# Three gate products in the woven groups of RWKV and six beside S5, instead of two and seven

## The chip, the cores and the metric

The kernel runs on one core of a Trainium2 chip. A core has five engines with instruction queues of their own: TensorE (PE, matrix products into PSUM banks; PEld is its loading of weights), VectorE (DVE), ScalarE (ACT), GpSimd (POOL) and SyncE (SP), which here issues nearly all DMA transfers. Engines wait for each other by semaphores. The metric is the device time of one execution in microseconds (us), the median of several. Lower is better.

## The reference, cut to what matters

The program is two layers of a network on 256 tokens of width 2048, in float32. The change lies in the second layer. It normalizes its input to `h`, projects it, and feeds three branches (GDN, RWKV, S5), which are merged under gates:

```python
h = rms_norm_2(x, norm_w[i])
proj = h @ w_in[i]
(g_qkv, g_z, g_b, g_a, r_feat, r_z, s_u, s_z, gate_logits) = _split_cols(proj, SPLIT_SIZES)
o_a = gdn_branch(...)      # gated delta rule, chunks of tokens
o_b = rwkv7_branch(...)    # state recurrence over tokens, 16 heads of 64
o_c = s5_branch(...)       # complex diagonal recurrence over 256 tokens
branch_proj = einsum('blnc,ncd->blnd', branches, w_branch[i])
gates = sigmoid(gate_logits.reshape(bsz, seq, N_BRANCH, D_MODEL) + gate_b[i])
merged = sum(gates * branch_proj, axis=2)
x = x + merged @ w_out[i]
```

The gates depend on `h` alone, so their products can be made at any time before the merge. They are 3 branches x 2048 columns; in chunks of 512 columns that is 12 gate products, each 256 tokens x 2048 x 512.

## The kernel before

The second layer runs as `stage_gdn`, `stage_rwkv`, `stage_s5`, `stage_merge`, one after the other. Within a stage the engines run `nc.Block`s: every engine has its list of instructions, and all engines meet at the end of a block. Nothing in a stage starts before the block ahead of it is over on every engine.

The class `Beside` makes products with the whole of `h` (kept in SBUF as `whole`, named `x_rows` in the profile) in small pieces beside the work of a stage. A job is one chunk of 512 columns: a gate product or one of the four chunks of the S5 input. It has 8 units; a unit is 2 row tiles x 2 slices of the contraction, 4 matmuls of 128x512, which the profile shows as 8 records since each float32 matmul is done in two passes. A gate job begins with two matmuls that put the bias into its two banks (4 records, L3244). `on_pe(pe, units)` is written out by hand in PE's program and issues so many units (L3249). A job takes two PSUM banks. When its last unit is done, `on_act` empties both on ACT (L3265, a sigmoid for gates), and SP stores the result to DRAM (L3216). The weights of a unit are one DMA (L3210) into a ring of 5 slots.

The 12 gate jobs are dealt out by two constants: `GATES_BESIDE_GDN = 3` in GDN, `GATES_BESIDE_RWKV = 2` in RWKV, and the other 7 in S5. The RWKV stage also makes the four S5 input chunks, so its list of jobs is three S5 chunks, the gate jobs, and the last S5 chunk.

The third block of `stage_rwkv` (called the woven block below) holds the RWKV recurrence as 4 groups (2 halves of the heads x 2 row tiles). A group needs the inverse of a triangular matrix (`Inverse`: `turn`, then five levels of `masked_products` and `update_products`, L3048 and L3059), and with it two chunks of recurrence (`key_state` L4035/L4036, `solved` L4044, `read_out` L4057 to L4066). PE weaves the recurrence of group n into the inverse of group n+1. Between them stand units of the jobs, by the table

```python
BEFORE_FIRST, IN_GROUP, BEHIND_LAST = 3, (1, 1), ((1, 1, 2), (1, 1, 1))
```

3 units before the first inverse; in each of the three groups one in slot 0 (before `solved(n, 0)`) and one in slot 1 (before level 5 of the inverse); and 4 + 3 in the six slots of the last group's recurrence, which has no inverse beside it. 3 + 6 + 7 = 16 units are 2 jobs. In this block the jobs have a ring of only two banks of their own (`banks[6:8]`, `beside.ring`), which is what one job takes; ACT also copies the inverse's products to SBUF (L3104).

`stage_s5` has a first block (coefficients, and one gate job on PE in three pieces) and a second, the recurrence. There PE makes the inputs of the recurrence (L4509), then `beside.on_pe(pe, (len(jobs) - 1) * Beside.UNITS)`, six gate jobs in a row, and then the output products (L4519), eight tiles of the state to a bank, four banks. DVE runs `s5_scan` meanwhile; its last loop goes in 8 steps over 4 tiles each (L4282 to L4289, 128x960), and each step raises `s_dve`, on which the output products wait. After the scan DVE reads the four banks (L4550), ACT applies GELU to the whole (L4533), and the block ends. The next block loads `s5_glu_w` (L240) and multiplies by it (L257).

Of the kernel before, what the change touches and what calls it, by code (L numbers as in the profile page):

```python
# [3269 lines left out]
def gate_jobs(io, gates_dram, lo, hi):  # L3270

    work = [(br, c) for br in range(BRANCHES) for c in range(D // CHUNK)][lo:hi]
    return [(io["w_in_2"][0], MG0 + br * D + c * CHUNK, io["gate_b_2"][0, br:br + 1, c * CHUNK:(c + 1) * CHUNK], ACT.Sigmoid,
             gates_dram[br, c]) for br, c in work]


GATES_BESIDE_GDN = 3
GATES_BESIDE_RWKV = 2

GDN_PARTS = (4, 3, 5, 4, 4, 2, 2)  # L3280

# [1 line left out]

SHIFT_UNITS = 10

BEFORE_FIRST, IN_GROUP, BEHIND_LAST = 3, (1, 1), ((1, 1, 2), (1, 1, 1))


GH, GD = 8, 128
# [431 lines left out]
def stage_rwkv(nc, m, io, st, whole, cols, s5_dram, gates_dram):  # L3721
    with ExitStack() as ctx:
# [20 lines left out]
        s5_jobs = [(io["w_in_2"][0], SU0 + c * CHUNK, None, ACT.Copy, s5_dram[c]) for c in range(4)]  # L3743
        rwkv_jobs = s5_jobs[0:3] + gate_jobs(io, gates_dram, GATES_BESIDE_GDN, GATES_BESIDE_GDN + GATES_BESIDE_RWKV) + s5_jobs[3:4]
        beside = Beside(m, st, ctx, "s5_in", whole, rwkv_jobs)
# [19 lines left out]
        with ExitStack() as c1:  # L3765
# [4 lines left out]
            with nc.Block() as block:  # L3770
                @block.sync
                def _(sp):

                    beside.load_units(sp, 2)
                    sp.wait_ge(fed_stored, 16 * (1 + TT * len(chunks(NP_, RWKV_WIDTH))))
                    for tt in range(TT):
                        sp.dma_start(prev[:, tt, :], fed[tt * P:(tt + 1) * P, 0:NR]).then_inc(shifted[tt], 16)
                    beside.load_units(sp, 3)
                    sp.dma_start(mu, everywhere(io["rwkv_mu_2"], NR)).then_inc(mu_loaded, 16)
                    beside.on_sp(sp, 1)  # L3780
                    sp.dma_start(wup[:, 0, :], io["rwkv_w_up_2"][0]).then_inc(up_loaded, 16)
                    sp.dma_start(wup[:, 1, :], io["rwkv_a_up_2"][0]).then_inc(up_loaded, 16)
                    for (row, name), landed in zip(rows_of, (r_loaded, r_loaded, kk_loaded, ka_loaded, rk_loaded)):
                        sp.dma_start(row, everywhere(flat(io[name]), HALF)).then_inc(landed, 16)
                    beside.load_units(sp, SHIFT_UNITS + 1)
                    beside.store(sp)
# [177 lines left out]
        with ExitStack() as c2:  # L3964
# [7 lines left out]
            groups = [(hg, tt) for hg in range(2) for tt in range(TT)]  # L3972
            with nc.Block() as block:
                @block.sync
                def _(sp):
                    beside.on_sp(sp, GATES_BESIDE_RWKV)
                    beside.load_units(sp, beside.at_unit + Beside.HELD)
# [7 lines left out]
                @block.scalar  # L3985
                def _(act):
                    for n in range(len(groups)):
                        inv.at(n)
                        if n == len(groups) - 1:
                            beside.on_act(act)  # L3990
                        for lv in range(1, inv.LEVELS + 1):
                            inv.copy_products(act, lv)
                    beside.on_act(act)

                @block.tensor
                def _(pe):
# [331 lines left out]
def stage_s5(nc, m, io, st, whole, cols, s5_dram, gates_dram):  # L4328
    with ExitStack() as ctx:
# [6 lines left out]
        par = m.sb(ctx, "s5_parity", [P, 2])  # L4336
        jobs = gate_jobs(io, gates_dram, GATES_BESIDE_GDN + GATES_BESIDE_RWKV, BRANCHES * (D // CHUNK))
        beside = Beside(m, st, ctx, "s5_gates", whole, jobs)
# [442 lines left out]
```

## Time and profile before

| | us |
|---|---|
| median of 3 runs | 3711.11 (3708.2 to 3716.0) |
| the profiled execution | 3712.48 |
| its span in the trace | 3710.5 |
| woven block of RWKV, from the first transposes to the last unit | 2859.0 to 3103.7 |
| second block of S5, from the first input product to the end of GELU | 3185.7 to 3399.2 |

In the whole span PE is busy 90%, DVE 70%, ACT 34%, POOL 11%. These are averages over stages with different limits. Times below are us from the start of the span. A row of the timeline gives start, duration, engine, line, operation, output and inputs, the shape, the number of instructions merged into the row, and in brackets how long the engine had been idle and for whom. A matmul's duration runs to the end of its pipeline, so neighbouring matmuls overlap a little, and the distance of two starts is the better price.

### The profile page before, as it was taken

Reading aid. Unit: us, or ns where it says so; the run is one execution under the profiler, and the core shown is the slowest. Engines: PE = TensorE matmul, PEld = TensorE weight load, DVE = VectorE, ACT = ScalarE, POOL = GpSimd, SP = SyncE. Lnnn points to the kernel's source line nnn. Section 1 sums busy time; section 2 is a strip of 40 time slices with the busy share of each in tenths; the row PEclk is TensorE's granted clock in tenths of the full one; section 3 lists DMA queues with packets and bytes.
Section 4 is the critical chain, followed back from the end, with each engine's and each line's share of the span. In section 5 each row is a group of like instructions: output and inputs, shape, how many; then the busy total and the mean of one; then the engine's idle time right before and its main releaser. Section 6 shows DMA issues by size and latency. Waiting matters only on the chain. (4 is left out here: it accounts for less than half of the span.)

```text
span 3710.5 us, 46494 instructions
## 1 busy us (share of the span) xinstructions
PE 3355.6 (90%) x18811; PEld 2618.5 (71%) x18811; DVE 2597.8 (70%) x3306; ACT 1267.8 (34%) x1467; POOL 410.6 (11%) x393
## 2 busy tenths in 40 slices
PE   7889878998889989999999799998989998999798
PEld 5756646788889989787877588567864764543676
DVE  5855768889999987687888754756446334894664
ACT  3322233334345555444444333313312010100333
POOL 0011101100121121232332100020000200000000
PEclk8888988999999999999999999999999989999899
DMA  9974367847989999899999564315563104453663
GB/s 355 379 266 131 115 221 286 304 166 257 328 317 368 364 352 353 334 380 373 366 379 385 220 209 155 115 41 169 199 219 108 42 19 118 149 152 103 206 230 147
DMA packets 294612, 870.29 MB, mean 235 GB/s; under 512 B 33584, under 2 KB 108436, under 8 KB 242432
## 3 DMA queue, kind: packets, MB, share of 16 engines
q1 hardware_dynamic: 257616, 670.64, 51.5%
q0 software_dynamic: 34320, 190.40, 13.6%
q10 hardware_dynamic: 2464, 6.29, 0.5%
q8 instruction: 149, 2.44, 0.3%
q14 instruction: 63, 0.52, 0.0%
HBM read 820.22 MB, written 46.38 MB: 234 GB/s over the span
## 5 line engine op out<-in xcount | busy, mean ns | idle before, releaser
L2493 DVE TENSOR_TENSOR expert_w_low<-expert_w,expert_w_high 128x2048 fp32r<-128x2048 f32 x256 | 585.4, 2287 | 154.3 <-ACT expert_w_high L2920 151.9
L2828 PE MATMUL bank<-h_halves,expert_w_high 128*128 128x384 f32 x2048 | 611.3, 369 | 64.8 <-DVE expert_w_low L2493 64.5
L2920 ACT ACTIVATE expert_w_high<-expert_w 128x2048 fp32r<-128x2048 f32 x256 | 490.4, 1916 | 449.7 <-DMA expert_w<-in_peer_v_dram 295.6
L298 DVE TENSOR_TENSOR weights_low<-weights,weights_high 128x1024 fp32r<-128x1024 f32 (+4 forms) x288 | 338.3, 1177 | 297.1 <-ACT weights_high L281 293.5
L2829 PE MATMUL bank<-h_halves,expert_w_low 128*128 128x192 f32 x2048 | 520.2, 254 | 0.0
L281 ACT ACTIVATE weights_high<-weights 128x1024 fp32r<-128x1024 f32 (+4 forms) x288 | 293.5, 1021 | 468.1 <-PE bank L326 384.7
L2828 PEld LDWEIGHTS bank<-h_halves,expert_w_high 128*128 128x128 f32 x2048 | 394.0, 192 | 75.3 <-DVE expert_w_low L2493 75.0
L2829 PEld LDWEIGHTS bank<-h_halves,expert_w_low 128*128 128x128 f32 x2048 | 400.6, 196 | 0.0
L2897 PE MATMUL bank<-expert_w_high,gated_acts_halves 128*128 128x512 f32 x512 | 203.4, 397 | 22.6 <-DVE expert_w_low L2493 22.5
L2898 PE MATMUL bank<-expert_w_low,gated_acts_halves 128*128 128x512 f32 x512 | 201.5, 394 | 0.0
L2899 PE MATMUL bank<-expert_w_high,gated_acts_halves 128*128 128x512 f32 x512 | 201.5, 393 | 0.0
L2901 PE MATMUL bank<-expert_w_high,gated_acts_halves 128*128 128x512 f32 x512 | 199.2, 389 | 0.0
L2902 PE MATMUL bank<-expert_w_low,gated_acts_halves 128*128 128x512 f32 x512 | 199.2, 389 | 0.0
L3249 PE MATMUL bank<-s_gates_w,x_rows 128*128 128x512 f32 x448 | 198.2, 603 | 0.4 <-DMA s_gates_w<-in_w_in_dram 0.4
L3249 PE MATMUL bank<-s_in_w,x_rows 128*128 128x512 f32 x384 | 185.2, 640 | 11.5 <-DMA s_in_w<-in_w_in_dram 8.8
L3249 PEld LDWEIGHTS bank<-s_gates_w,x_rows 128*128 128x128 f32 x448 | 85.5, 192 | 111.2 <-issue 109.9
L3249 PEld LDWEIGHTS bank<-s_in_w,x_rows 128*128 128x128 f32 x384 | 77.0, 205 | 111.0 <-issue 96.3
L2789 POOL DMA_INDIRECT query_area<-in_peer_v_dram,own_list x43 | 114.8, 2671 | 260.1 <-DVE choose_area L2549 253.1
L1495 PE MATMUL bank<-weights,x_rows 128*128 128x512 f32 (+1 forms) x256 | 121.9, 630 | 18.6 <-DMA weights<-in_w_in_dram 15.3
L324 PE MATMUL bank<-weights_high,branch_high 128*128 128x512 f32 x320 | 127.7, 399 | 11.4 <-DVE weights_low L298 6.8
L2897 PEld LDWEIGHTS bank<-expert_w_high,gated_acts_halves 128*128 128x128 f32 x512 | 97.3, 190 | 50.5 <-issue 30.7
L326 PE MATMUL bank<-weights_high,branch_low 128*128 128x512 f32 x320 | 125.8, 393 | 0.0
(740 smaller groups left out, 6508.1 us busy)
## 6 DMA issues: line engine op xcount, KB each, us to landing
expert_w<-in_peer_u_dram SPq DMA_DIRECT2D x128, 1024.0 KB
expert_w<-in_peer_v_dram SPq DMA_DIRECT2D x128, 1024.0 KB
weights<-in_ada_w_dram SPq DMA_DIRECT2D x88, 512.0 KB, 9.3
weights<-in_w_out_dram SPq DMA_DIRECT2D x32, 1024.0 KB, 13.3
weights<-in_w_in_dram SPq DMA_DIRECT2D x32, 960.0 KB, 9.1
weights<-in_w_in_dram SPq DMA_DIRECT2D x32, 928.0 KB, 9.8
weights<-in_w_in_dram SPq DMA_DIRECT2D x56, 512.0 KB, 7.1
s_gates_w<-in_w_in_dram SPq DMA_DIRECT2D x56, 512.0 KB, 3.7
```

The costliest lines, as they stand in the source:

```text
L281: act.activation(self.high[:, u % self.UNITS_HELD, :, 0:n], self.buf[b][:, k:k + self.UNIT, 0:n], ACT.Copy).then_inc(self.high_ready, 1)
L298: dve.tensor_tensor(self.low[:, u % self.UNITS_HELD, :, 0:n], self.buf[b][:, k:k + self.UNIT, 0:n], self.high[:, u % self.UNITS_HELD, :, 0 ...
L2493: dve.tensor_tensor(wl[:, n % RING, :], w_sb[:, n % RING, :], wh[:, n % RING, :], ALU.subtract).then_inc(wl_ready, 1)
L2828: pe.matmul(o[:, 0:2 * DENSE], uh[:, b, k, :], acts.both[:, k, :, 0:DENSE], start=(k == 0), stop=False)
L2829: mm = pe.matmul(o[:, DENSE:2 * DENSE], ul[:, b, k, :], acts.h[:, k, 0:DENSE], start=False, stop=(k == KD - 1))
L2897: pe.matmul(bank[:, :], high, wh[:, b, cs], start=first, stop=False)
L2898: pe.matmul(bank[:, :], high, wl[:, b, cs], start=False, stop=False)
L2899: mm = pe.matmul(bank[:, :], low, wh[:, b, cs], start=False, stop=last)
L2901: pe.matmul(bank[:, :], both, wh[:, b, cs], start=first, stop=False)
L2902: mm = pe.matmul(bank[:, :], both, wl[:, b, cs], start=False, stop=last)
L2920: act.activation(wh[:, n % RING, :], w_sb[:, n % RING, :], ACT.Copy).then_inc(wh_ready, 1)
L3249: mm = pe.matmul(self.both[tt][:, :], self.whole[:, p * self.UNIT + u, tt * P:(tt + 1) * P], self.w[:, n % self.HELD, u, :], start=first, ...
```

## The change

One gate job goes from the second block of S5 to the woven block of RWKV. The 8 units are put where the table says: one more in both slots of each of the three groups, and one more in the first slot of each of the two chunks behind the last group. The list becomes 3 + 12 + 9 = 24 units, 3 jobs. ACT empties the first job's banks one group earlier, and two jobs at the end.

```diff
 GATES_BESIDE_GDN = 3
-GATES_BESIDE_RWKV = 2
+GATES_BESIDE_RWKV = 3
...
-BEFORE_FIRST, IN_GROUP, BEHIND_LAST = 3, (1, 1), ((1, 1, 2), (1, 1, 1))
+BEFORE_FIRST, IN_GROUP, BEHIND_LAST = 3, (2, 2), ((2, 1, 2), (2, 1, 1))
...
                 def _(act):
                     for n in range(len(groups)):
                         inv.at(n)
-                        if n == len(groups) - 1:
+                        if n == len(groups) // 2:
                             beside.on_act(act)
                         for lv in range(1, inv.LEVELS + 1):
                             inv.copy_products(act, lv)
-                    beside.on_act(act)
+                    for _job in range(GATES_BESIDE_RWKV - 1):
+                        beside.on_act(act)
```

What else follows from the constants: the woven block's SP list has one job more (8 weight loads, a bias load, a store) and the second block of S5 one less. The diff adds one line, so lines of the RWKV and S5 stages beyond it are one higher after the change (L4044 is L4045).

PE in the first woven group, slot 0 and what follows it (L4015 are the key products, L4044 is `solved`, L3059 `turn`, L3048 the first level). Here x4 counts matmuls, of which the trace shows two records each. Before:

```order
9916 L4015 MATMUL bank<-weights_3 64x128 x16
9917 L4036 MATMUL bank<-rwkv_rows,weights_3 64x64 x8
9918 L4015 MATMUL bank<-weights_3 64x128 x16
9919 L3249 MATMUL bank<-s_in_w,x_rows 128x512 x4
9920 L4044 MATMUL bank<-rwkv_xu,weights_3 64x64 x8
9921 L3059 MATMUL bank<-block_ident,weights_3 64x64 x16
9922 L3048 MATMUL bank<-weights_3 64x64 x16
```

PE in the same place of the changed kernel:

```order
9916 L4016 MATMUL bank<-weights_3 64x128 x16
9917 L4037 MATMUL bank<-rwkv_rows,weights_3 64x64 x8
9918 L4016 MATMUL bank<-weights_3 64x128 x16
9919 L3249 MATMUL bank<-s_in_w,x_rows 128x512 x8
9920 L4045 MATMUL bank<-rwkv_xu,weights_3 64x64 x8
9921 L3059 MATMUL bank<-block_ident,weights_3 64x64 x16
9922 L3048 MATMUL bank<-weights_3 64x64 x16
```

Two units stand where one was, and nothing else moved.

PE in slot 0 of the second woven group of the changed kernel, where the first job ends and the second begins in the same slot:

```order
10051 L4016 MATMUL bank<-weights_3 64x128 x16
10052 L3249 MATMUL bank<-s_in_w,x_rows 128x512 x4
10053 L3244 MATMUL bank<-s_in_bias,incl_mask 128x512 x2
10054 L3249 MATMUL bank<-s_in_w,x_rows 128x512 x4
10055 L4045 MATMUL bank<-rwkv_xu,weights_3 64x64 x8
```

Before, a job ended in one slot and the next began in another; now two ends of jobs lie within a slot, here and in the first slot behind the last group.

ACT in the woven block of the changed kernel (L3104 copies the inverse's products, ten to a group; L3265 empties a job's two banks):

```order
665 L3104 ACTIVATE rwkv_products<-bank 128x256 x20
666 L3265 ACT_TABLE_LOAD
667 L3265 ACTIVATE s_in_out<-bank 128x512 x2
668 L3104 ACTIVATE rwkv_products<-bank 128x256 x20
669 L3265 ACTIVATE s_in_out<-bank 128x512 x4
```

The first emptying stood behind 30 copies and stands now behind 20; two stand at the end, where one was.

PE at the end of the S5 recurrence of the changed kernel (L4520 are the output products, L4519 before the change):

```order
10408 L3244 MATMUL bank<-s_gates_bias,incl_mask 128x512 x2
10409 L3249 MATMUL bank<-s_gates_w,x_rows 128x512 x32
10410 L3244 MATMUL bank<-s_gates_bias,incl_mask 128x512 x2
10411 L3249 MATMUL bank<-s_gates_w,x_rows 128x512 x32
10412 L4520 MATMUL bank<-weights_3,s_C_T 32x256 x64
```

Five such pairs of rows stand ahead of the output products, where six were.

## Rows read from the trace of the kernel before

**Rows 1.** Stretches: bounds, length, busy us of each engine (instructions), PE's granted clock, DMA.

```profile
core 0: us, PE busy (x) PEld busy (x) DVE busy (x) ACT busy (x) POOL busy (x), PEclk, DMA share, GB/s
2904.00:3104.00 200.00, 191.59 (x2586) 136.56 (x2576) 60.44 (x124) 14.75 (x35) 22.22 (x18) 0.91 0.13 36
```

**Rows 2.** Timeline of PE in the first woven group.

```profile
2903.67 1.10 PE L4015 MATMUL bank<-weights 64*64 64x128 f32 x32 [0.23 <-DVE weights L4129]
2904.70 3.70 PE L3249 MATMUL bank<-s_in_w,x_rows 128*128 128x512 f32 x8
2908.33 1.08 PE L4044 MATMUL bank<-rwkv_xu,weights 64*64 64x64 f32 x15
...
2917.68 0.68 PE L3048 MATMUL bank<-weights,rwkv_products 64*64 64x64 f32 x16 [0.99 <-DVE rwkv_K L4170]
...
2940.01 5.76 PE L3249 MATMUL bank<-s_in_w,x_rows 128*128 128x512 f32 x8
2945.71 1.15 PE L3048 MATMUL bank<-weights,rwkv_last_masked 64*64 64x64 f32 x32
```

**Rows 3.** Timeline of DVE around slot 0 of the same group.

```profile
2904.80 0.68 DVE L4141 TENSOR_SCALAR rwkv_xu<-bank 64x512 f32<-64x512 f32 x1
2905.62 1.29 DVE L4120 TENSOR_TENSOR weights<-bank,block_masks 128x512 f32<-128x512 f32 x2
2909.51 0.68 DVE L4147 COPY rwkv_xu<-bank 64x512 f32<-64x512 f32 x1 [2.60 <-PE bank L4044]
```

**Rows 4.** Timeline of PE: one whole gate job beside the S5 recurrence, and the next.

```profile
3201.36 27.73 PE L3249 MATMUL bank<-s_gates_w,x_rows 128*128 128x512 f32 x64
3229.35 1.95 PE L3244 MATMUL bank<-s_gates_bias,incl_mask 1*128 1x512 f32 x4 [0.26 <-issue]
3231.23 27.73 PE L3249 MATMUL bank<-s_gates_w,x_rows 128*128 128x512 f32 x64
```

**Rows 5.** Timeline of PE between two jobs in the two-bank ring, second block of RWKV.

```profile
2830.31 27.70 PE L3249 MATMUL bank<-s_in_w,x_rows 128*128 128x512 f32 x64 [0.73 <-ACT s_in_out L3265]
```

**Rows 6.** Timeline of ACT: the first woven job is emptied.

```profile
3004.70 1.28 ACT L3265 ACT_TABLE_LOAD   x1 [6.02 <-PE bank L3249]
3006.00 1.08 ACT L3265 ACTIVATE s_in_out<-bank 128x512 f32<-128x512 f32 x2
```

**Rows 7.** Timeline of PE in the third group's slot 1 and behind the last group.

```profile
3037.75 3.77 PE L3244 MATMUL bank<-s_in_bias,incl_mask 1*128 1x512 f32 x4
3041.46 6.24 PE L3249 MATMUL bank<-s_in_w,x_rows 128*128 128x512 f32 x8
...
3055.73 5.93 PE L3249 MATMUL bank<-s_in_w,x_rows 128*128 128x512 f32 x8
...
3073.65 8.94 PE L3249 MATMUL bank<-s_in_w,x_rows 128*128 128x512 f32 x16
```

**Rows 8.** Timeline of PE at the end of the S5 recurrence.

```profile
3354.12 27.73 PE L3249 MATMUL bank<-s_gates_w,x_rows 128*128 128x512 f32 x64
3382.11 14.09 PE L4519 MATMUL bank<-weights,s_C_T 128*32 128x256 f32 x128 [0.26 <-issue]
```

**Rows 9.** Timeline of DVE in the same stretch.

```profile
3368.12 1.16 DVE L4282 TENSOR_TENSOR s_tmp_dve<-s_powers,s_carry 128x960 f32<-128x960 f32 x1
...
3375.86 1.15 DVE L4289 TENSOR_TENSOR weights<-weights,s_tmp_dve 128x960 f32<-128x960 f32 x1
3385.88 0.87 DVE L4550 SCALAR_TENSOR_TENSOR branch_columns<-s_u_columns,vector_columns,bank 128x256 f32<-128x256 f32 x2 [8.87 <-PE bank L4519]
...
3396.28 0.87 DVE L4550 SCALAR_TENSOR_TENSOR branch_columns<-s_u_columns,vector_columns,bank 128x256 f32<-128x256 f32 x2 [2.60 <-PE bank L4519]
```

**Rows 10.** Timeline of ACT behind that.

```profile
3397.24 1.91 ACT L4533 ACTIVATE branch_columns<-branch_columns 128x2048 f32<-128x2048 f32 x1 [13.37 <-DVEq L4553]
```

**Rows 11.** Timeline of PE in the block after it.

```profile
3403.25 16.53 PE L257 MATMUL bank<-weights,branch_columns 128*128 128x512 f32 x32 [7.05 <-DMA weights<-in_s_glu_w_dram]
3420.07 13.97 PE L257 MATMUL bank<-weights,branch_columns 128*128 128x512 f32 x32 [0.29 <-issue]
```

**Rows 12.** Stretches of PE's clock as it falls idle behind the output products.

```profile
3392.00:3396.00 4.00, 4.00 (x40) 1.00 0.00 0
3396.00:3400.00 4.00, 0.20 (x4) 0.77 0.00 0
3400.00:3404.00 4.00, 0.75 (x1) 0.50 0.88 277
```

## The prediction

> **What bounds the kernel now.** The change takes work from one place and puts it in another, so two places decide, and I read each for the engine that ends last. The table of the whole span (PE 90% busy) does not answer this; the stretches and the timelines do.
>
> First the S5 recurrence, where a job is taken away. Read the ends. PE starts its sixth gate job at 3354.12, which takes 27.73, and starts the output products at 3382.11 [rows 8]. DVE ends the last step of the recurrence at 3375.86 + 1.15 = 3377.0 and then waits 8.87 for PE's first bank [rows 9]. So PE is late, by 3382.1 - 3377.0 = 5.1 us at the start of the output products, and the products themselves (14.09) then run wholly behind the recurrence, though three quarters of them need only steps that had long ended. The chain there is: PE gate jobs, PE output products, DVE's last bank (ends 3396.28 + 0.87 = 3397.15 [rows 9]), GELU at 3397.24 [rows 10], end of the block.
>
> Then the woven block of RWKV, where the job goes. In the 200 us from 2904 to 3104 PE is busy 191.6, DVE 60.4, ACT 14.8, POOL 22.2 [rows 1]. PE is the bound, with only 8.4 us idle. What the reader should look for is whether this idle time lies where the new units stand. It does not. In slot 0 of the first group PE comes to the unit after the key products, runs it in 3.63 us from start to start (2904.70 to 2908.33), and goes on to `solved` without a gap [rows 2]. What `solved` waits for, DVE's negated rows, was ready at 2904.80 + 0.68 = 2905.5, and DVE had finished the value rows too (2905.62 + 1.29 = 2906.9) and sat idle 2.60 until PE's `solved` [rows 3]. The one unit already covers all that DVE had to do. In slot 1 the unit is followed by level 5 without a gap (2940.01, then 2945.71) [rows 2]. PE's waits in a group, 0.99 us for DVE before an update being the largest [rows 2], come further behind a unit, in a ping-pong of PE, ACT and DVE that starts anew after it, and a longer unit only shifts them.
>
> **What the change moves, term by term.**
>
> Units in the woven block. A whole job of 8 units takes 27.73 us [rows 4], 27.73 / 8 = 3.47 for a unit that directly follows another one; all 8 new units do. 8 x 3.47 = 27.7 us, all on PE's path. With the bias: two matmuls, from 3229.35 to 3231.23, 1.9 us [rows 4].
>
> Ends of jobs inside a slot. The two-bank ring makes PE wait until ACT has emptied both banks. The same ring cost 0.73 us between two jobs in the block before [rows 5]. There ACT needed no table load; here the first emptying is a sigmoid with a load of 1.28 ahead of it, on an ACT that had been idle for 6.02 [rows 6]. The first bank is full half a unit (1.7 us) before the second, so the load lies in that time. I take 0.73 twice, 1.5 us; bounds 1.1 (hardly more than the drain of 0.26 that every end has [rows 4] and one emptying) and 4.1 (two waits of 0.73, and two times 1.28 if the load or ACT's queue is not covered). Nothing else hangs on ACT there: its copies for the group ahead are done, those of the next come later.
>
> DMAs on SP: eight weight loads, a bias load and a store more in the woven block. The DMA engines are 13% busy there [rows 1], and a ring of five slots runs ahead of PE. Nothing, hidden behind PE's own units; if a load came late it would show as a PE wait, which no unit of the woven block has in the trace.
>
> Sum for RWKV: 27.7 + 1.9 + 1.5 = +31.1 us.
>
> S5. Without the sixth job PE is through 29.9 us earlier (3201.36 to 3231.23 is one job with bias and drain [rows 4]), at 3352.2. Then DVE is late: the recurrence does not depend on PE and still ends at 3377.0. A step of its last loop takes 8.9 us (3368.12 to 3377.0 [rows 9]) and an eighth of the products 14.09 / 8 = 1.8 [rows 8], so by 3377.0 the products of seven of eight steps are done, and after it PE has the last eighth left, 1.8 us at full clock. DVE meanwhile takes the first three banks, 0.87 each, then the fourth. The end is the later of DVE alone, 3377.1 + 4 x 0.87 = 3380.6, and PE's last eighth, 0.1 for the signal, 1.8 and 0.87 of DVE, 3379.8. At half the clock PE's eighth is 3.5 and the end 3381.5. Against 3397.15 that is 16.5 or 15.6 us. Which one? PE will have been idle for most of the 14 us ahead of it. The row for that: when PE fell idle at 3396.2 the clock went from 1.00 to 0.77 in the slice in which it stopped and to 0.50 (1.2 GHz) in the next [rows 12]. So I take the lower clock and 15.6. On this point the Trainium skill speaks against counting the full gain: "TensorE: Matmul & The Clock Gate", part 1, says that the throttled clock is the default and that only activity lifts it; the trace agrees as far as [rows 12] go, and by the rule the gain is 15.6, without it 16.5.
>
> Behind it: the load of the GLU weights is issued when the block is over, so the whole chain moves up. The first half of the GLU product took 16.53, the second 13.97, the difference 2.6 being the start at the low clock [rows 11]. It starts cold before and after; I count no difference, with +-1 us as bound. The scan itself, in DVE alone, keeps its time.
>
> Sum: +31.1 - 15.6 = **+15.5 us**. The profiled execution took 3712.48, its span 3710.5, with 2.0 around it that no edit touches; so 3728.0 for such an execution. It lies 1.4 above the median of the three runs. For the median: 3711.11 + 15.5 = **3726.6 us**, 0.42% slower. A job of 29.9 us is taken from a place that can give only half of it back, since the recurrence becomes the bound there, and put where PE has no idle time for it.
>
> **Rivals.**
>
> *The clock is kept up in RWKV (not slower).* The woven block runs at a mean clock of 0.91. Between the two levels of 1.2 and 2.4 GHz that is (1 - 0.91) x 2 x 200 = 36 us at the lower one. Slots with a dense unit came out at 5.76 [rows 2], 6.24 and 5.93 us [rows 7] instead of 3.70, and a bias pair at 3.77 [rows 7] instead of 1.9. The clock falls in long runs of small 64-wide products and comes back during a unit. If twice as many units keep it up, time comes back: at most half of the 36 us, 18, if everything in it were bound by columns. Then the block pays 31.1 - 18 = 13.1, and the total is -2.5: 3708.6, inside 0.2%. If a third comes back (6), it is 3720.6. The page named above has this rule too, activity releases the throttle, and by it a denser block should have fewer low stretches. What the rows say against it: the falls come far behind a unit, in read-out and key-state products whose length the change leaves alone; two units back to back still met one (8.94 instead of 3.63 + 3.47 = 7.1 [rows 7]). It decides for "not slower" from 8.1 us given back, for "faster by over 0.2%" only from 23, more than its ceiling.
>
> *The new units run at the low clock (slower still).* If the low stretches last through the whole slot, a new unit costs about 5.9 instead of 3.47, 2.4 more. For all eight that is +19 (3746), for half of them, those in slot 1 and the first behind, +10: 3736. Against it: two units in one slot took 8.94, not 12 [rows 7].
>
> *S5 gives less.* PE is late at the start of the output products by 5.1 us, and that much comes back in any case; the other 10.5 come back only if the products of the early steps do run during the recurrence. If half of that failed, 10 us would come back and the time is 3732. No row names what could hold them up: the four banks of this ring are empty and the weights are in SBUF.
>
> *The units fill waits after all.* If all 8.4 us of idle PE in the woven block were used up, the sum is +7.1 and the time 3718. [rows 2, 3] show the waits elsewhere.
>
> **How the numbers follow.** The sum as forecast, with the woven cost between 26 and 36: 0.66. Clock kept up by 6 us or more: 0.15 (of it 0.10 within 0.2%, 0.02 faster, 0.03 slower). Units at the low clock: 0.12. S5 gives less: 0.05. Waits filled: 0.02. A measurement of this kernel can tell about 0.2% (7.4 us) from no change. So faster 0.02, same 0.12, slower 0.86. The range reaches from 3716 (a clock that gives back 10 of its 18) to 3737 (half of the new units at the low clock); outside lie the rest of the first rival and the far end of the second, some 0.15 together.
>
> **What the profile after would show.** Right: in slots 0 and 1 rows of 16 records instead of 8, some 7.1 us long and up to 9.5 at a low clock, followed at once by the next products; the stretch from the first transposes to the last unit longer by about 31 us, with PE's idle time in it near 8 to 10 us; two waits of about 0.7 for ACT (L3265) on PE; in S5 PE idle between 3352 and 3377 on the old scale, rows of the output products split by waits for DVE, DVE's four readings right behind the recurrence, and GELU 15 to 16 us earlier relative to the first input product. Wrong: a mean clock in the woven block near 1.00, or PE's idle time in it fallen to a few us, or a recurrence that itself takes another time. If the woven block grew by less than 24 us, the first term is wrong; if S5 shrank by less than 13, the last.

## The result: 17.4 us slower

| | us |
|---|---|
| median before (14 runs beside the changed kernel) | 3710.28 (3693.71 to 3724.80) |
| median after (14 runs) | 3729.89 (3712.38 to 3738.59) |
| ratio after / before | 1.0047, 95% interval 1.0031 to 1.0063 |
| the profiled execution of after, and its span | 3718.94, 3717.0 |

The ratio is +17.4 us (11.5 to 23.4) on 3710.28; the forecast was +15.5 and a median of 3726.6. The measured median is 3.3 above the forecast, inside its range.

The two profiled executions differ by only 6.5 us in span. So the span as a whole must not be read; the stages must. The stages are cut at six starts that both traces have: the first transposes of the woven block (L371, `rwkv_K`), the next block's first unit, the transposes behind that block's job (L371 again), the first input product and GELU in S5's second block, and the transposes behind the GLU (L371, `s_y_rows`).

| us | before | after | difference |
|---|---|---|---|
| all that lies ahead of the woven block | 2859.0 | 2847.9 | -11.1 |
| woven block of RWKV | 245.8 | 279.4 | +33.6 |
| last block of RWKV | 28.0 | 28.0 | 0.0 |
| S5, first block | 52.8 | 55.0 | +2.2 |
| S5, second block up to GELU | 211.6 | 194.7 | -16.9 |
| GELU and GLU | 49.7 | 48.8 | -0.9 |
| the rest | 263.5 | 263.2 | -0.3 |

The code ahead of the woven block is the same in both kernels, and that part took 2845 to 2859 us in the traces of this case, whatever the kernel. So the 11 us lie inside the spread between executions, and they hid that much of the loss. From the woven block to the end the trace gives +17.6, and the runs give +17.4. How well a single trace can carry that is looked at under "The same again".

### The profile page after: what moved, and what is told of

Its sections match the earlier page's. It is cut to its first block and busy times, and to the rows that moved or that the text cites. A ratio compares the mean times of both kernels' runs of the same rounds, so it can differ in the third digit from the quotient of the medians.

```text
span 3717.0 us, 46494 instructions
## 1 busy us (share of the span) xinstructions
PE 3360.2 (90%) x18811; PEld 2623.0 (71%) x18811; DVE 2598.2 (70%) x3306; ACT 1267.2 (34%) x1467; POOL 410.5 (11%) x393
## 5 line engine op out<-in xcount | busy, mean ns | idle before, releaser
L3249 PE MATMUL bank<-s_in_w,x_rows 128*128 128x512 f32 x448 | 212.4, 632 | 12.1 <-DMA s_in_w<-in_w_in_dram 9.4
L3249 PEld LDWEIGHTS bank<-s_in_w,x_rows 128*128 128x128 f32 x448 | 88.7, 202 | 125.5 <-issue 110.1
L3249 PE MATMUL bank<-s_gates_w,x_rows 128*128 128x512 f32 x384 | 174.1, 615 | 0.0
L3249 PEld LDWEIGHTS bank<-s_gates_w,x_rows 128*128 128x128 f32 x384 | 74.9, 197 | 98.1 <-issue 98.0
L324 PE MATMUL bank<-weights_high,branch_high 128*128 128x512 f32 x320 | 127.3, 398 | 11.6 <-DVE weights_low L298 6.8
```

What stands on the lines that cost most here:

```text
L3249: mm = pe.matmul(self.both[tt][:, :], self.whole[:, p * self.UNIT + u, tt * P:(tt + 1) * P], self.w[:, n % self.HELD, u, :], start=first, ...
```

## The profile after

The head of the page of after: span, and busy time of each engine.

```profile
span 3717.0 us, 46494 instructions
PE 3360.2 (90%) x18811; PEld 2623.0 (71%) x18811; DVE 2598.2 (70%) x3306; ACT 1267.2 (34%) x1467; POOL 410.5 (11%) x393
```

Nothing of the change can be read from these shares. The woven block can be read as a stretch (length, busy time of PE, PEld, DVE, ACT, POOL, PE's clock, DMA), first in the trace of before and then in that of after:

```profile
2859.00:3104.90 245.90, 233.15 (x3273) 167.32 (x3273) 84.46 (x170) 18.92 (x45) 29.61 (x24) 0.92 0.17 49
```

```profile
2847.90:3127.30 279.40, 266.48 (x3340) 183.69 (x3341) 84.41 (x170) 20.13 (x47) 29.59 (x24) 0.91 0.19 60
```

PE's idle time is 245.9 - 233.15 = 12.75 us before and 279.4 - 266.48 = 12.92 after. The added work went on top of everything else. The groups of PE's instructions in that block show of what it consists. Before:

```profile
L3249 PE MATMUL bank<-s_in_w,x_rows 128*128 128x512 f32 x129 | 69.4, 691 | 1.2 <-PEq L3973 1.2
L4065 PE MATMUL bank<-rwkv_xu,weights 64*64 64x64 f32 x128 | 20.5, 247 | 0.0
L4044 PE MATMUL bank<-rwkv_xu,weights 64*64 64x64 f32 x128 | 9.0, 220 | 0.3 <-issue 0.3
L3244 PE MATMUL bank<-s_in_bias,incl_mask 1*128 1x512 f32 x8 | 5.8, 854 | 0.0
```

And after:

```profile
L3249 PE MATMUL bank<-s_in_w,x_rows 128*128 128x512 f32 x192 | 98.1, 667 | 0.0
L4066 PE MATMUL bank<-rwkv_xu,weights 64*64 64x64 f32 x128 | 21.4, 256 | 0.0
L4045 PE MATMUL bank<-rwkv_xu,weights 64*64 64x64 f32 x128 | 9.0, 220 | 0.0
L3244 PE MATMUL bank<-s_in_bias,incl_mask 1*128 1x512 f32 x12 | 5.9, 608 | 1.6 <-ACT s_in_out L3265 1.6
```

One of the 129 records of before belongs to the next block's unit (0.7 us), so the units went from 68.7 to 98.1, +29.4 us for 64 records. The bias went from 5.8 to 5.9 only, since one of its pairs had fallen into a low-clock stretch before [rows 7] and none did after. The new waits for ACT are 1.6 us.

The timeline of PE in the slots of after: slots 0 and 1 of the first group, slot 0 of the second group, where a job ends within the slot (its bias, with the wait), slot 1 of the third group, and the second end of a job, in the first slot behind the last group.

```profile
2893.54 7.13 PE L3249 MATMUL bank<-s_in_w,x_rows 128*128 128x512 f32 x16
2900.60 1.08 PE L4045 MATMUL bank<-rwkv_xu,weights 64*64 64x64 f32 x15
...
2932.91 8.70 PE L3249 MATMUL bank<-s_in_w,x_rows 128*128 128x512 f32 x16
...
2949.75 3.70 PE L3249 MATMUL bank<-s_in_w,x_rows 128*128 128x512 f32 x8
2954.30 1.95 PE L3244 MATMUL bank<-s_in_bias,incl_mask 1*128 1x512 f32 x4 [0.85 <-ACT s_in_out L3265]
2956.18 5.40 PE L3249 MATMUL bank<-s_in_w,x_rows 128*128 128x512 f32 x8
...
3051.01 9.38 PE L3249 MATMUL bank<-s_in_w,x_rows 128*128 128x512 f32 x16
...
3075.02 1.95 PE L3244 MATMUL bank<-s_in_bias,incl_mask 1*128 1x512 f32 x4 [0.73 <-ACT s_in_out L3265]
```

The first row answers to the unit of [rows 2]: 2893.54 to 2900.60 is 7.06 us instead of 3.63, and `solved` follows without a gap. 7.1 us is a pair at the high clock; 8.70 and 9.38 are pairs that met a low stretch, as the 8.94 of [rows 7].

The end of the S5 recurrence in after, PE and then DVE and ACT:

```profile
3378.55 10.61 PE L4520 MATMUL bank<-weights,s_C_T 128*32 128x256 f32 x96 [0.26 <-issue]
3392.69 1.94 PE L4520 MATMUL bank<-weights,s_C_T 128*32 128x256 f32 x16 [3.54 <-DVEq L4546]
3401.62 1.96 PE L4520 MATMUL bank<-weights,s_C_T 128*32 128x256 f32 x16 [6.99 <-DVEq L4546]
```

```profile
3400.37 1.15 DVE L4290 TENSOR_TENSOR weights<-weights,s_tmp_dve 128x960 f32<-128x960 f32 x1
3401.67 3.22 DVE L4551 SCALAR_TENSOR_TENSOR branch_columns<-s_u_columns,vector_columns,bank 128x256 f32<-128x256 f32 x8
```

```profile
3404.97 1.91 ACT L4534 ACTIVATE branch_columns<-branch_columns 128x2048 f32<-128x2048 f32 x1 [24.67 <-DVEq L4554]
```

In [rows 8] PE was late and did all the products in one row behind the recurrence. Now it has done six of eight parts early and waits for the scan before each of the last two; DVE reads the four banks in 3.22 us without a gap, where it waited 8.87 and 2.60 for PE in [rows 9]. From the end of the last step (3401.52) to GELU it is 3.5 us; before it was 3397.24 - 3377.01 = 20.2. The difference is 16.8 us.

## The experiments

The ratios are against before, from runs beside it on the same chip. Where a stage is named, its length comes from the trace of that kernel. Lengths of the two blocks in every trace, and what remains of the span from the woven block on:

| kernel | woven block | S5, second block | woven block to end |
|---|---|---|---|
| before | 245.8 | 211.6 | 851.5 |
| after | 279.4 | 194.7 | 869.1 |
| rwkv_alone | 279.3 | 213.2 | 885.7 |
| s5_alone | 245.3 | 194.6 | 837.9 |
| one_heap | 276.6 | 194.7 | 864.8 |
| unwoven1 | 245.6 | 213.3 | 851.7 |
| s5_two_less | 246.1 | 194.7 | 832.6 |
| change_again | 285.7 | 194.7 | 875.9 |
| rwkv_alone2 | 282.8 | 213.3 | 892.8 |

### The two halves apart

**rwkv_alone.** The woven block of the change, with seven jobs in S5 as before. Nothing of the result is left out; S5 makes one gate product a second time, into memory that nobody reads. The cut shows what it adds to the changed kernel.

```diff
 GATES_BESIDE_RWKV = 3
 BEFORE_FIRST, IN_GROUP, BEHIND_LAST = 3, (2, 2), ((2, 1, 2), (2, 1, 1))
...
+        spare = m.dram("spare_gate", [P, TT, CHUNK])
+        jobs = [jobs[0][:4] + (spare[:, :, :],)] + jobs
```

> The RWKV half of the change alone: three gate jobs in the woven block as after the change, and still seven in S5 (one of them is made a second time, into a spare buffer). Theory: PE bounds the woven block and nothing covers the eight new units, so it grows as it did after the change (33.6 us between the first transposes and the next block's first unit; 31.1 by the sum ahead of the result), and S5 gives nothing back: slower by 33 us, ratio 1.009. Rival (the new units fill waits and half of the cost of the change comes from elsewhere): slower by under 20 us.

Measured: 1.0116 (1.0096 to 1.0136), 3750.43 against 3708.87; that is +43 us (36 to 50). Its trace gives +34.2 from the woven block to the end, with the woven block at 279.3.

**s5_alone.** The code of before, with one gate job fewer in S5. It leaves out the last of the twelve gate products; the merge reads its neighbour instead (the second pair of lines), so the merge does the same work.

```diff
-        jobs = gate_jobs(io, gates_dram, GATES_BESIDE_GDN + GATES_BESIDE_RWKV, BRANCHES * (D // CHUNK))
+        jobs = gate_jobs(io, gates_dram, GATES_BESIDE_GDN + GATES_BESIDE_RWKV, BRANCHES * (D // CHUNK) - 1)
...
-                    sp.dma_start(gate[:, i % 3, :, :], gates_dram[br, c // CHUNK]).then_inc(gate_loaded[i % 3], 16)
+                    sp.dma_start(gate[:, i % 3, :, :], gates_dram[br, min(c // CHUNK, 2) if br == 2 else c // CHUNK]).then_inc(gate_loaded[i % 3], 16)
```

> The S5 half alone: two gate jobs in RWKV as before the change, six in S5; the last gate product is left out, and the merge reads its neighbour in its place. Theory: the recurrence on DVE becomes the bound and only about 16 us of a job's 29.9 come back: faster by 15.6 to 17 us, ratio 0.9955, DVE reading the four banks right behind its last step. Rival (PE's output products are held up otherwise): faster by 5 to 10 us. Rival (a job is worth its whole time): faster by 30.

Measured: 0.9946 (0.9929 to 0.9964), 3688.50 against 3708.87; -20 us (-26 to -13). The stages give -13.6, with the S5 block at 194.6 and a first block of S5 that took 57.4 instead of 52.8; the edit leaves that block alone, and it took 55.0 and 55.8 in other traces.

The two halves together give 43 - 20 = +23 by the medians and 34.2 - 13.6 = +20.6 by the stages, against 17.4 and 17.6 for the whole. The woven block and the second block of S5 are each the same whether the other half is there or not (279.4 and 279.3, 194.7 and 194.6). Without the edit the S5 block took 211.5 to 213.3, so its part is 17 to 18.6 us. Two of the medians lie farther out than the stages; **rwkv_alone2** looks at that again below.

### Does it matter how the third job is put in?

**one_heap.** The third job stands as a heap of eight more units ahead of the first group; the slots keep one unit each. ACT's emptying is moved to match. The cut is against the kernel before.

```diff
-GATES_BESIDE_RWKV = 2
+GATES_BESIDE_RWKV = 3
...
-BEFORE_FIRST, IN_GROUP, BEHIND_LAST = 3, (1, 1), ((1, 1, 2), (1, 1, 1))
+BEFORE_FIRST, IN_GROUP, BEHIND_LAST = 11, (1, 1), ((1, 1, 2), (1, 1, 1))
...
-                        if n == len(groups) - 1:
+                        if n in (0, len(groups) - 1):
                             beside.on_act(act)
```

> The change with its eight new units in one heap ahead of the first inverse, where nothing waits beside them, and the table of the groups as before it (one unit to a slot). ACT empties the first job ahead of the first group's copies. Theory (the second unit of a slot covers nothing): the same as the change, slower than before by 15 to 19 us; a little less, by the 2 us that low-clock stretches and one end of a job cost in the slots. Rival (weaving covers waits): the heap is slower than the change by 5 us or more.

Measured: 1.0023 (1.0007 to 1.0039), +8.5 us (2.6 to 14.5). That is less than the 15 to 19 us expected; the trace gives +13.3 from the woven block to the end. The woven block grew by 30.8, not by 33.6. Of the 2.8 less, 1.6 lie in the units (96.5 us instead of 98.1; 97.1 below holds one record of the next block) and 0.8 in the wait for ACT, which comes once instead of twice; the bias (+1.8) and the small products (-1.8) cancel. The stretch in this kernel,

```profile
2859.40:3136.10 276.70, 264.91 (x3341) 181.96 (x3341) 84.46 (x170) 20.13 (x47) 29.61 (x24) 0.92 0.19 61
```

and the two groups:

```profile
L3249 PE MATMUL bank<-s_in_w,x_rows 128*128 128x512 f32 x193 | 97.1, 658 | 1.2 <-PEq L3973 1.2
L3244 PE MATMUL bank<-s_in_bias,incl_mask 1*128 1x512 f32 x12 | 7.7, 772 | 0.8 <-ACT s_in_out L3265 0.8
```

A heap that lies beside nothing costs no more than eight units woven in. So the weaving of the third job hides none of it. If anything the heap is cheaper: its units run one behind the other at a granted clock of 1.00, and the units cost 27.8 us more than before, where the woven ones cost 29.4 here and 35.9 in a second trace below.

**unwoven1.** The two jobs of before, with the six units of the groups' slots put ahead of the first group too.

```diff
-BEFORE_FIRST, IN_GROUP, BEHIND_LAST = 3, (1, 1), ((1, 1, 2), (1, 1, 1))
+BEFORE_FIRST, IN_GROUP, BEHIND_LAST = 9, (0, 0), ((1, 1, 2), (1, 1, 1))
...
-                        if n == len(groups) - 1:
+                        if n == 0:
```

> The kernel before with the six units of the groups' slots (one each) taken out and put ahead of the first inverse, so that the groups hold none. Theory: the first unit of a slot does cover something, since DVE works for 1 to 2.3 us from PE's arrival at slot 0 and for about 3 at slot 1, which then shows as PE waits: slower than before by 3 to 12 us, PE idle in the woven block up by as much. Rival (no unit of a slot covers anything): the same time within 2 us. Together with the change this gives the worth of no, one and two units to a slot.

Measured: 1.0001 (0.9988 to 1.0015), and a woven block of 245.6 against 245.8. I had expected it to be 3 to 12 us slower, since the prediction reads [rows 2, 3] as a unit that covers DVE's work. It does cover it, but the wait that it covers is short. PE in slot 0 of the first group, without a unit between the key products and `solved`:

```profile
2917.10 1.10 PE L4015 MATMUL bank<-weights 64*64 64x128 f32 x32 [0.23 <-DVE weights L4129]
2919.02 1.08 PE L4044 MATMUL bank<-rwkv_xu,weights 64*64 64x64 f32 x15 [0.81 <-DVEq L4142]
```

The wait of 0.81 us is all that a unit of 3.6 us hides there; before `solved` PE waits 1.6 us in the whole block, and PE's idle time in it is 12.2 us against 12.7 before.

That the length is the same does not mean that the six units left no trace. PE's stretch from the start of the first inverse on, first before and then here, and this kernel's units as a group:

```profile
2884.30:3104.88 220.58, 209.66 (x3118) 153.66 (x3117) 70.54 (x147) 18.92 (x45) 22.22 (x18) 0.91 0.13 38
```

```profile
2898.90:3095.56 196.66, 187.07 (x3064) 150.73 (x3065) 70.32 (x147) 16.52 (x42) 22.25 (x18) 0.88 0.08 24
L3249 PE MATMUL bank<-s_in_w,x_rows 128*128 128x512 f32 x128 | 61.0, 632 | 0.0
```

The units cost 7.7 us less than in the kernel before (61.0 against 68.7) and the bias pairs 1.9 less (3.9 against 5.8), since more of them ran at the high clock. PE's other work took as much longer, some 10 us (168.5 against 158.6), in groups whose granted clock was 0.88 where it had been 0.91. These two cancel. **For the length of this block the table of the slots decides hardly anything: PE's work is its length, and moving units only moves who meets the low clock.** This rests on one trace of unwoven1; the medians agree that the time is the same.

### How much can S5 give?

**s5_two_less.** As s5_alone, with two jobs fewer: the last two of the twelve gate products are left out, and the merge reads another one in their places.

```diff
-        jobs = gate_jobs(io, gates_dram, GATES_BESIDE_GDN + GATES_BESIDE_RWKV, BRANCHES * (D // CHUNK))
+        jobs = gate_jobs(io, gates_dram, GATES_BESIDE_GDN + GATES_BESIDE_RWKV, BRANCHES * (D // CHUNK) - 2)
...
```

> The kernel before with two gate jobs fewer beside the S5 recurrence (five in S5; the last two gate products are left out, and the merge reads their neighbour). Theory: with one job fewer DVE's recurrence is already the bound of that block, so the second one fewer gives nothing: the block from the first input product to GELU takes 194.6 us as with one fewer (211.6 before), and the time is 17 us below before, no more. Rival (PE still bounds part of the block): another 5 to 30 us.

Measured: 0.9917 (0.9894 to 0.9941), 3683.90 in four runs. The block is 194.7 us, as with one job fewer. PE and ACT at its end:

```profile
3357.29 1.96 PE L4519 MATMUL bank<-weights,s_C_T 128*32 128x256 f32 x16 [7.16 <-DVEq L4545]
3366.22 1.96 PE L4519 MATMUL bank<-weights,s_C_T 128*32 128x256 f32 x16 [6.98 <-DVEq L4545]
```

```profile
3369.57 1.91 ACT L4533 ACTIVATE branch_columns<-branch_columns 128x2048 f32<-128x2048 f32 x1 [56.20 <-DVEq L4553]
```

The second job fewer gives nothing in its block: the scan sets the end, and with one job fewer PE already waits 3.54 and 6.99 us for it. The medians show -31 us (-39 to -22), and the block explains -16.9 of it; the trace's other stages from the woven block on give -2.0 more, to -18.9 in all. The trace does not show where the rest of the -31 comes from; there are only four runs.

### The same again

The woven block of before took 245.3 to 246.1 us in the five traces that have its units where they were. To see how firm the 279.4 is, the change itself and rwkv_alone were run once more.

**change_again** is the changed kernel, unaltered.

> The changed kernel once more, beside its RWKV half alone on the same chip. The stages of the traces add to 17.6 us over the kernel before: ratio 1.0047. Its woven block 279.4 us and its S5 block 194.7 in the trace.

Measured: 1.0045 (1.0029 to 1.0061), +16.7 us: the result stands. But its trace has a woven block of 285.7, 6.3 us longer, at a mean clock of 0.90. Its stretch, its units as a group, and some of its slots in the timeline:

```profile
2846.80:3132.50 285.70, 272.15 (x3341) 184.79 (x3341) 84.41 (x170) 20.12 (x47) 29.61 (x24) 0.90 0.19 59
```

```profile
L3249 PE MATMUL bank<-s_in_w,x_rows 128*128 128x512 f32 x193 | 105.3, 704 | 1.2 <-PEq L3973 1.2
```

```profile
2994.34 9.91 PE L3249 MATMUL bank<-s_in_w,x_rows 128*128 128x512 f32 x16
...
3067.04 5.97 PE L3249 MATMUL bank<-s_in_w,x_rows 128*128 128x512 f32 x8
...
3073.75 2.45 PE L3244 MATMUL bank<-s_in_bias,incl_mask 1*128 1x512 f32 x4 [0.73 <-ACT s_in_out L3265]
3076.13 6.55 PE L3249 MATMUL bank<-s_in_w,x_rows 128*128 128x512 f32 x8
```

More of the slots fell into low-clock stretches: 9.91 instead of 7.1 for a pair, 5.97 and 6.55 instead of 3.6 for single units. The units took 104.6 us (105.3 less the one record of the next block) where the same code took 98.1. The small products did not grow: none of their larger groups took longer than in the first trace (L4066, for one, 21.2 us against 21.4).

**rwkv_alone2** is rwkv_alone, unaltered.

> The RWKV half alone once more. Its first measurement was 1.0116 (1.0096 to 1.0136), 43 us, where the stages of its trace add to 34.2. If the stages tell the whole of it, the ratio is 1.009 now, and the difference to the changed kernel 17 us. If the half alone costs something ahead of RWKV that one trace does not show, the ratio is again near 1.0116 and the difference 25 us.

Measured: 1.0095 (1.0076 to 1.0114), +35 us (28 to 42), so the first +43 was probably some 8 us too high, which its interval (36 to 50) allows. Its trace gives +41.3 from the woven block on, with a woven block of 282.8 and a first block of S5 3.0 us longer than before; the first trace gave 34.2. A single trace of a kernel with three woven jobs is good to some 7 us. The distance to the change is 35 - 17 = 18 us, close to S5's part, 16.9 by the block.

### A version that is faster than both

The same units stand in GDN, too. In the block of GDN's recurrence four of them stand at the start (`GDN_PARTS[4]`), and DVE waits 10.24 us there for PE's first product; at the end PE waits 7.69 us for the last rows, with nothing to do. PE and DVE before, at the end and at the start:

```profile
2537.84 3.68 PE L371 MATMUL bank<-ident,gdn_rows 128*128 128x128 f32 x16 [7.69 <-DVEq L3700]
...
2546.11 0.74 PE L324 MATMUL bank<-weights_high,h_rwkv_high 128*128 128x480 f32 x1 [4.59 <-DVE h_rwkv_low L566]
```

```profile
2434.18 1.89 DVE L3628 COPY weights<-bank 128x512 f32<-128x512 f32 x3 [10.24 <-PE bank L3544]
```

**gdn_tail** moves two of the four units from the start to the end, ahead of that wait. ACT empties the job at the end, and its store goes behind the weight loads on SP.

```diff
-GDN_PARTS = (4, 3, 5, 4, 4, 2, 2)
+GDN_PARTS = (4, 3, 5, 4, 2, 2, 2, 2)
...
-                    beside.finish_sp(sp)
                     sp.wait_ge(o_ready, TT)
                     m.weights.load(sp, io["w_in_2"][0], RF0, RWKV_WIDTH)
+                    beside.finish_sp(sp)
...
-                        if c == TT - 1:
-                            beside.on_act(act)
...
+                    beside.on_act(act)
...
+                    beside.on_pe(pe, GDN_PARTS[7])
                     pe.wait_ge(o_done, 1)
```

> The kernel before, all computed, with two units of the third GDN gate job moved within GDN: out of the four ahead of the recurrence's block, where DVE waits 10.2 us for PE, and in front of the final transposes, where PE waits 7.7 us for DVE. ACT's emptying of that job and its store move to the end, behind the load of the RWKV weights. Theory (a unit costs nothing only where PE waits): faster by 6 to 7 us, ratio 0.998. Rival (a unit is worth the same everywhere): no change. Rival (the late store holds the block's end up): slower by 2 to 4.

Measured: 0.9978 (0.9964 to 0.9992), -8 us (-13 to -3), 3705.40 against 3712.63. PE at the end of that block and at the start of the next, the store on SP's queue, and DVE at the start:

```profile
2516.13 7.03 PE L3249 MATMUL bank<-gdn_gates_w,x_rows 128*128 128x512 f32 x16
2523.97 1.97 PE L371 MATMUL bank<-ident,gdn_rows 128*128 128x128 f32 x16 [0.82 <-DVEq L3700]
...
2535.56 0.74 PE L324 MATMUL bank<-weights_high,h_rwkv_high 128*128 128x480 f32 x1 [9.61 <-DVE h_rwkv_low L566]
```

```profile
2523.97 0.34 SPq L3216 DMA_DIRECT2D merge_gates<-gdn_gates_out  x1
```

```profile
2420.65 1.89 DVE L3628 COPY weights<-bank 128x512 f32<-128x512 f32 x3 [3.38 <-PE bank L3543]
```

The wait at the start fell by 6.9 and the units lie in what was idle time (7.69 to 0.82). But half of it is lost again behind it: from the last transposes to the next block's first product it takes 11.6 instead of 8.3 us, since the block is not over before the late store has landed (SP waits for it in `finish_sp`). The store is issued at 2523.97 and takes 7.6 us to land, and SP's first DMA of the next block is issued at 2532.12. In the trace the stage as a whole became only 0.5 us shorter (214.3 to 213.8), with 3.4 us more in an earlier part at a lower clock.

**gdn_tail_b** is the same with one unit more at the start of the stage, and one fewer in the third part.

```diff
-GDN_PARTS = (4, 3, 5, 4, 2, 2, 2, 2)
+GDN_PARTS = (5, 3, 4, 4, 2, 2, 2, 2)
```

> The same, and one unit of GDN's first block moved from its third piece (five units, behind which DVE waits 8.7 us) to its first, behind which PE waits 3.0 us in three places. Theory: another 3 us, faster than before by 9 to 10 us, ratio 0.9975. Rival (the first piece then delays DVE's softplus chain): no more than the run without it.

Measured: 0.9981 (0.9966 to 0.9995), -7 us (-13 to -2); its stage took 211.0. The 3 us more that were expected of it did not show; the two can't be told apart. Both are faster than before by 0.2%, and than the change by more. The stage explains only part of that: 0.5 us of 8 in the one trace and 3.3 of 7 in the other. Where the rest comes from is not shown.

## Why the prediction was right, point by point

**Units in the woven block: 27.7 forecast, 29.4 measured** in the trace of after (35.9 in that of change_again, by the groups). All lie on PE's path, as forecast. The step price of 3.47 us holds at the high clock: 2893.54 to 2900.60 is 3.63 + 3.43. What was missing is the clock. For woven units a forecast at the price of a dense job is the lower edge: some of them will fall into stretches at 1.2 GHz.

**Bias: 1.9 forecast, 0.1 in the trace.** The added pair cost 1.95, and another got cheaper by 1.8, having left a low stretch.

**Two ends of jobs inside a slot: 1.5 forecast, 0.85 + 0.73 = 1.6 measured.** The row of an idle ring at another place [rows 5] was a good price. The first end has 0.12 more, and a table load comes before its emptying; that the load is the cause is not shown.

**What the sum had left out: 3.8 us of small products.** PE's busy time grew by 33.3, the units and the bias by 29.5. The rest is spread over the read-out and key-state products, such as L4066 (20.5 to 21.4), and those of the inverse (L3048, where the three largest groups went from 69.4 to 71.5). At a mean clock of 0.92 over 245.9 us the block of before spent (1 - 0.92) x 2 x 245.9 = 39 us at 1.2 GHz, that of after at 0.91 some 50, so more low time fell on them too; the rounding of the clock is worth 2.5 us in these figures. The idle time stood at 12.9, with the 1.6 of new waits in it, so 1.4 of the old waits were filled.

**S5: 15.6 forecast, 16.9 measured.** The step that was a little off is the choice between 16.5 and 15.6. I took the lower clock at the last eighth to mean twice its time, 3.5 us. The clock was at the lower level, 1.2 GHz, as PE's stretches of after show (length, busy times, then the clock):

```profile
3392.00:3396.00 4.00, 1.94 (x16) 0.59 (x16) 3.86 (x5) 0.00 (x0) 0.00 (x0) 0.68 0.01 4
3400.00:3404.00 4.00, 1.96 (x16) 0.63 (x16) 3.85 (x8) 0.00 (x0) 0.00 (x0) 0.50 0.00 0
```

But the eighth took 1.96 us there, as it had taken 1.94 where the clock was 0.68 on average, and 14.09 / 8 = 1.76 in the unbroken row of before [rows 8]. So DVE was the later one, and its four banks (3.22) set the end. On this point "TensorE: Matmul & The Clock Gate", part 1, of the Trainium skill was right that an idle TensorE falls back to the throttled clock (0.50 in the row above), and I drew too much from it: these products did not take twice as long for that.

**The GLU: no difference forecast, -0.9 measured**, inside the bound of 1. The first half took 15.49 where it was 16.53 in [rows 11].

**The rivals.** *The clock is kept up* did not come true for the second unit of a slot: the mean clock was 0.91 and 0.90, not higher than the 0.92 of before, and the small products took more time, not less. Its mechanism is not empty, though. Without the first unit (unwoven1) the groups ran at 0.88 instead of 0.91 and their small products took longer, which cancelled what the units had gained outside. *The new units run at the low clock* holds in part: it was worth 2 to 8 us of the 19 it could have cost, by execution. The ceiling of 19 was itself too low. The 5.9 us a unit that it goes by were units only partly at the low clock (0.59 to 0.64 on average over the rows of 5.76 to 6.24); a unit wholly at 1.2 GHz would take 2 x 3.63 = 7.3 us, an estimate from the last section's rows. *S5 gives less* is refuted, since the products of the early steps ran during the recurrence (the row of 96). *The units fill waits* is refuted but for 1.4 us, and one_heap says the same: without any cover the job costs 30.8.

**How much of the closeness is luck.** The sum of after's stages is 33.6 - 16.9 = +16.7, and +0.9 from the small stages. The mechanism held in both places, but the 2 us between forecast and trace are what is left of misses that partly cancel: units +1.7, bias -1.8, waits +0.1, small products +3.8, old waits filled -1.4, S5 -1.3, small stages +0.9. In change_again the woven block grew by 39.9 us, beyond the 26 to 36 that the forecast allowed for it. That the woven cost varies by 6 us between executions while the ratios of two measurements agree (1.0047 and 1.0045) leaves open which of the two traces is the usual one; the medians speak for a sum of 17.

## What to carry to other kernels

Independent work is free only where the engine that does it waits. Before moving it, find for both places which engine ends last, and from what point another takes over: here a job of 30 us was worth 17 where the recurrence stood behind it, nothing from the second job on, and its full price plus waits where PE was the bound. A place with an instruction between two dependent ones is not proof that something is hidden: take the instruction away, or find the wait that it covers (here 0.8 us). And when a time stays the same, look whether its parts did: unwoven1 kept its length because units got cheaper by as much as other products got dearer. And where the span as a whole varies more than the edit is worth, compare stage by stage and add up.

## What the runs showed of the hardware

**A low granted clock does not slow all matmuls alike.** Rows as stretches, with the mean granted clock as the third number from the end: a woven unit of change_again (512 columns; 3.70 us at 1.00); key-state products of after, 18 records and then 14 (the x counts take in neighbours that overlap); and output products of S5 (256 columns into 32 rows) in s5_two_less, 32 records and then 16.

```profile
3067.04:3073.01 5.97, 5.97 (x9) 2.32 (x8) 0.68 (x1) 0.60 (x1) 0.00 (x0) 0.61 0.00 0
3063.47:3065.78 2.31, 2.31 (x18) 1.71 (x18) 0.00 (x0) 0.00 (x0) 0.00 (x0) 1.00 0.00 0
3065.78:3068.61 2.83, 2.83 (x17) 2.01 (x15) 0.00 (x0) 0.00 (x0) 0.00 (x0) 0.50 0.00 0
3311.60:3315.30 3.70, 3.67 (x32) 1.20 (x32) 3.56 (x4) 1.68 (x2) 0.00 (x0) 1.00 0.35 142
3330.10:3332.10 2.00, 1.96 (x16) 0.63 (x16) 1.94 (x2) 0.00 (x0) 0.00 (x0) 0.50 0.00 0
```

For the unit time and clock trade one for one: 5.97 x 0.61 = 3.6. A bias pair, also 512 columns, took 3.77 us at 0.50 [rows 7] and 1.95 at 1.00. The 64-wide key-state products went from 0.13 to 0.20 us a record, 1.6 times. The narrow output products were not slowed at all: 3.67 us for 32 records at 1.00 and 1.96 for 16 at 0.50. What bounds them instead is not shown.

**One unit in each slot went with a higher clock than none, a second did not.** Without units in the groups (unwoven1) the clock from the first inverse on was 0.88, with one 0.91 (0.90 in one_heap), with two 0.91 and 0.89 (change_again). The kernels with one and two units can't be told apart by this, and each figure is of one trace. The mean clock alone does not give the length of the block either: unwoven1 had 0.90 over the whole of it at 245.6 us, before 0.92 at 245.8. What varies between executions is how many units fall into the low stretches. A block with 16 units, woven as before, was stable within 1 us (245.3 to 246.1), and one with 24 woven ones took 279.3 to 285.7.
